# Moving the value convolution of a gated linear attention from VectorE to GpSimd

## What is computed

```python
p = h @ w_in
qkv = silu(centred_dwconv(p[..., :n_qkv], conv_w))     # 5 taps along the tokens, one weight per channel
q = l2norm(q) * DN_DK ** -0.5;  k = l2norm(k);  v = v
...
a_low = where(strict, (k * beta) @ k.T * gamma, 0)      # per chunk of 64 tokens
uw = triangular_solve(eye + a_low, [v * beta, k * beta * exp(G)])
...
for each chunk, in both directions:
    v_new = u_n - w_n @ s
    o_n = q_dec @ s + (q @ k.T * gamma) @ v_new
    s = s * exp(g_last) + k_dec.T @ v_new
```

## Time and profile before

| | us |
|---|---|
| median of 3 runs (3764.49 to 3772.21) | 3769.91 |
| the profiled execution, its own time | 3767.85 |
| its span, first to last instruction | 3766.2 |
| TensorE busy in the span | 3461.8 |
| VectorE busy | 915.3 |
| ScalarE busy | 488.1 |
| GpSimd busy | 108.7 |

### The profile page before, as it was taken

One profiled execution on the slowest core, in us unless ns is written; L12 is line 12 of the kernel. 1 busy time (PEld: TensorE's weight loads), 2 busy tenths in 40 slices (PEclk: granted clock), 3 DMA queues, 4 the chain that ended last, 5 costly groups with the idle time before them and its releaser, 6 DMA issues.

```text
span 3766.2 us, 45281 instructions
## 1 busy us (share of the span) xinstructions
PE 3461.8 (92%) x18441; PEld 2572.2 (68%) x18467; DVE 915.3 (24%) x1917; ACT 488.1 (13%) x1138; POOL 108.7 (3%) x118
## 2 busy tenths in 40 slices
PE   7999987899897997996889987789999999999998
PEld 4555665577575775775756766568888888888886
DVE  1677775300101332004740002210100000000001
ACT  1322321100001221002121011110000000000000
POOL 0111120000000000000000000000000000000000
PEclk8999999999999998998989998889999999999999
DMA  6444312253444223532013432258888888888885
GB/s 207 146 169 173 135 47 79 99 161 107 156 146 160 68 68 101 167 104 96 34 45 123 150 126 76 61 167 302 269 283 286 271 298 272 285 285 273 297 273 199
DMA packets 475303, 636.71 MB, mean 169 GB/s; under 512 B 11182, under 2 KB 419357, under 8 KB 467877
## 3 DMA queue, kind: packets, MB, share of 16 engines
q1 hardware_dynamic: 469645, 612.49, 49.0%
q0 software_dynamic: 5536, 22.51, 1.8%
HBM read 633.75 MB, written 1.20 MB: 169 GB/s over the span
## 4 chain that ended last, share of the span: by engine, by line
PE 83%; DVE 7%; DVEq 2%; issue 2%; ACT 2%; DMA 2%; PEld 1%; PEldq 1%; ACTq 0%; SPq 0%; POOL 0%
PE PS L652 37%; PE PS L660 18%; PE PS L985 4%; PE PS L2917 2%; PE PS L506 2%; PE PS L1532 2%; PE PS L1528 1%; PE PS L1868 1%; DMA WO<-in_ada_w 1%; PE PS L1114 1%; PE PS L277 1%; ACT XT L481 1%; PE PS L3156 1%; DVE scratch L1384 1%; PE PS L1525 1%
## 5 line engine op out<-in xcount | busy, mean ns | idle before, releaser
L679 DVE TENSOR_TENSOR scratch<-scratch,PS 128x128 f32<-128x128 f32 (+1 forms) x312 | 101.6, 326 | 1994.2 <-ACT scratch L669 1994.2
L652 PEld LDWEIGHTS PS<-scratch,WO 128*128 128x128 f32 x3584 | 417.8, 192 | 53.6 <-issue 53.6
L652 PEld LDWEIGHTS PS<-scratch,WF 128*128 128x128 f32 x3584 | 409.0, 192 | 24.1 <-issue 22.9
L652 PE MATMUL PS<-scratch,WO 128*128 128x128 f32 x3584 | 418.2, 275 | 0.0
L652 PE MATMUL PS<-scratch,WF 128*128 128x128 f32 x3584 | 409.2, 275 | 0.0
L660 PE MATMUL PS<-WF,scratch 128*128 128x512 f32 x832 | 382.7, 592 | 0.0
L669 ACT ACTIVATE scratch<-PS 128x128 f32<-128x128 f32 (+1 forms) x312 | 96.0, 308 | 2001.3 <-PE PS L652 2001.3
L660 PE MATMUL PS<-WO,scratch 128*128 128x512 f32 x768 | 342.1, 592 | 0.0
L652 PE MATMUL PS<-XT,WF 128*128 128x256 f32 x1536 | 338.4, 381 | 0.0
L652 PEld LDWEIGHTS PS<-XT,WF 128*128 128x128 f32 x1536 | 294.2, 192 | 49.9 <-issue 10.1
L652 PE MATMUL PS<-XT,WO 128*128 128x256 f32 x1280 | 282.8, 379 | 0.0
(11 more groups left out here) (530 smaller groups left out, 3114.0 us busy)
## 6 DMA issues: line engine op xcount, KB each, us to landing
WF<-in_moe_wg SPq DMA_DIRECT2D x56, 1024.0 KB, 5.1
WF<-in_moe_wu SPq DMA_DIRECT2D x56, 1024.0 KB, 7.6
WF<-in_moe_wd SPq DMA_DIRECT2D x56, 1024.0 KB, 4.9
WO<-in_moe_wg SPq DMA_DIRECT2D x56, 1024.0 KB, 5.1
WO<-in_moe_wu SPq DMA_DIRECT2D x56, 1024.0 KB, 7.7
WO<-in_moe_wd SPq DMA_DIRECT2D x56, 1024.0 KB, 7.3
WO<-in_ada_w SPq DMA_DIRECT2D x48, 1024.0 KB, 6.6
WF<-in_ffn_w_gate SPq DMA_DIRECT2D x18, 1024.0 KB, 5.5
```

The lines of the kernel that those rows point to most:

```text
L652: mm = nc.tensor.matmul(k.PS[:, 4 + f, w * n:(w + 1) * n], slot.gu[:, w, kb, f * P:(f + 1) * P], rhs(kb), start=kb == 0, stop=kb == KB - 1)
L679: k.nc.vector.tensor_tensor(hid[:, f, :], sg[:, f, :], k.PS[:, 4 + f, n:2 * n], ALU.mult).then_inc(*slots[s].dve.done(f"h{f}"))
```

## The change

VectorE's five instructions per head for v go away (first tap L1279, then L1281 four times). GpSimd makes the convolution in a new function, directly after `bsel`: the first tap as a product into the destination `k.cv[:, 2]`, each further tap as a product into `k.vtap` (row 6 of the output tile OT, which is free until late) and an addition. That is 9 instructions with 512 columns per head, and a drain behind each. Who waited for VectorE's `convv` (ScalarE's SiLU of v, and its copy of pv into the same raw buffer two heads later) now waits for GpSimd's. Before its first instruction GpSimd waits for the copy of pv and, for f > 0, for the transpose of the previous v; for f = 0, for the constants and for `convqk`.

```diff
--- before.py
+++ after.py
@@ -864,8 +864,8 @@
     k.gdp_act = Steps(k, "gdp_act", "pq pk pv pz")
     k.gdf_pe = Steps(k, "gdf_pe", "ssq kk qk tk tv")
     k.gdf_act = Steps(k, "gdf_act", "silu z gam eg norm v ktok vb")
-    k.gdf_dve = Steps(k, "gdf_dve", "convqk gam sq convv unit gb at qg")
-    k.gdf_pool = Steps(k, "gdf_pool", "rows bsel qt")
+    k.gdf_dve = Steps(k, "gdf_dve", "convqk gam sq unit gb at qg")
+    k.gdf_pool = Steps(k, "gdf_pool", "rows bsel convv qt")
     k.gdi_pe = Steps(k, "gdi_pe", f"g00 g01 {products} {scan_pe}")
     k.gdi_dve = Steps(k, "gdi_dve", f"pt {levels} f0 f1 {scan_dve}")
     k.gdo_pe = Steps(k, "gdo_pe", "oss")
@@ -892,6 +892,7 @@
     k.st = wf.take(2, P)
     k.rr, k.vn = s.take(2, P), s.take(2, P)
     k.os, k.osq = s.take(512), s.take(512)
+    k.vtap = k.OT[:, HEADS - 2, :]
     k.gs = [k.stage[:, 0:512].rearrange("p (n c) -> p n c", n=4), k.OT[:, HEADS - 1, :].rearrange("p (n c) -> p n c", n=4)]
     k.tmp = k.sq[:, 0, :].rearrange("p (n c) -> p n c", n=4)
     k.gdn_w = [k.WH[:, n, :].rearrange("p (kb c) -> p kb c", kb=KB) for n in range(4)]
@@ -938,6 +939,27 @@
                 elif h + 1 < ADA_HEADS:
                     ada_unit_sync(k, sp, h + 2, 0)
             gdn_weights(k, sp, h + 3, n)
+
+
+def gdn_value_gpsimd(k, pool, f):
+
+    nc = k.nc
+    cv = k.cv[:, 2, :].rearrange("p (s c) -> p s c", s=2)
+    part = k.vtap.rearrange("p (s c) -> p s c", s=2)
+    pool.wait_ge(*k.gdp_act.at("pv", f))
+    if f:
+        pool.wait_ge(*k.gdf_pe.at("tv", f - 1))
+    else:
+        pool.wait_ge(*k.pre_act.at("vecs"))
+        pool.wait_ge(*k.gdf_dve.at("convqk", f))
+    for a in range(5):
+        raw = k.raw[f % 2][:, 2, :, a:a + L]
+        i = nc.gpsimd.tensor_scalar(part if a else cv, raw, conv_col(k, a, 2, f), None, ALU.mult)
+        pool.drain()
+        if a:
+            i = nc.gpsimd.tensor_tensor(cv, cv, part, ALU.add)
+            pool.drain()
+    pool.drain().then_inc(*k.gdf_pool.done("convv"))
 
 
 def gdn_gpsimd(k, pool):
@@ -959,6 +981,7 @@
         nc.gpsimd.tensor_tensor(k.gb.rearrange("p n c -> p (n c)"), k.rows[:, 2, :], k.rows[:, 3, :], ALU.add
                                 ).then_inc(*k.gdf_pool.done("bsel"))
         pool.drain()
+        gdn_value_gpsimd(k, pool, f)
         pool.wait_ge(*k.gdf_dve.at("qg", f))
         if f >= 2:
             pool.wait_ge(*k.gdi_pe.at("os31", f - 2))
@@ -999,7 +1022,7 @@
         a = act.activation(k.zs[:, h % 3, :], bank, ACT.Copy)
     else:
         if h >= 2:
-            act.wait_ge(*k.gdf_dve.at("convv" if name == "pv" else "convqk", h - 2))
+            act.wait_ge(*(k.gdf_pool.at("convv", h - 2) if name == "pv" else k.gdf_dve.at("convqk", h - 2)))
         a = act.activation(k.raw[h % 2][:, n, :, 2:258], bank.rearrange("p (s c) -> p s c", s=2), ACT.Copy)
     a.then_inc(*k.gdp_act.done(name))
 
@@ -1231,7 +1254,7 @@
         act.wait_ge(*T.at("ssq", f))
         rsqrt(k, act, k.sq, ps[:, 6:8, :], 1.0, k.eps[:, E_RMS:E_RMS + 1]).then_inc(*S.done("norm"))
         silu_table(act)
-        act.wait_ge(*V.at("convv", f))
+        act.wait_ge(*k.gdf_pool.at("convv", f))
         act.activation(k.cv[:, v, :], k.cv[:, v, :], ACT.Silu).then_inc(*S.done("v"))
         roots_table(act)
         raw("pv")
@@ -1351,7 +1374,6 @@
         gdn_taps(k, dve, f, (0, 1), range(5), "convqk")
         gdn_decay_vector(k, dve, f)
         gdn_squares_vector(k, dve, f)
-        gdn_taps(k, dve, f, (2,), range(5), "convv")
         gdn_unit_vector(k, dve, f)
         for name in ("at", "qg"):
             gdn_grams_vector(k, dve, f, name)
@@ -1401,12 +1423,8 @@
                 gdn_decay_vector(k, dve, f)
             if h:
                 gdn_out_vector(k, dve, h - 1, "out")
-        if l == 4:
-            if front:
-                gdn_squares_vector(k, dve, f)
-                gdn_taps(k, dve, f, (2,), (0, 1))
-        if l == 5 and front:
-            gdn_taps(k, dve, f, (2,), (2, 3, 4), "convv")
+        if l == 4 and front:
+            gdn_squares_vector(k, dve, f)
         if l == 6 and front:
             gdn_unit_vector(k, dve, f)
     for half in range(2):
```

## The result

| us | before | after |
|---|---|---|
| median of 4 runs on the same chip | 3767.49 (3764.49 to 3772.21) | 3792.61 (3790.59 to 3793.32) |
| profiled execution, its own time | 3767.85 | 3793.32 |
| its span | 3766.2 | 3791.5 |

After takes 1.0065 times as long as before, with a 95% interval of 1.0047 to 1.0082: 25 us more. The forecast was 31.5 more, so the sign and the range held and the sum was some 6 us too high.

The account below looks back on a forecast made before the run. The prediction took TensorE to bound the linear attention, with VectorE late at levels 1 to 3. Its terms, 16.5 + 5.3 + 5.3 + 7 - 2.6 = 31.5 us on 3767.85, gave 3800 us, range 3772 to 3834.

Parts of the forecast that it names:

- Length and price of a product: GpSimd's 512-column product with a per-channel weight: 0.95 us long, costing VectorE 0.6 us where it meets a victim.
- its own duration less 0.35: What a GpSimd instruction costs a VectorE instruction with two SBUF inputs that it meets; 0.95 us for one of 1.3.
- rival of long products: Products of 2.08 us also fill the second stream and level 3's masks: 60 us and more, 3828 to 3850; chance 0.12.
- Price of an addition: Each GpSimd addition of 1.3 us that meets a victim costs VectorE 0.95 us.
- heads 1 to 5: Levels 1 to 3 of these heads' preparation: VectorE's held taps and masks make TensorE wait, 3.3 us each, 16.5 in all.
- first stream: First four q and k taps of a head: they meet an addition, a product and an addition, losing 2.5 us.
- second stream: Second four q and k taps: one addition left, 0.95 us, of which VectorE's idle time takes 0.7; loss 0.3.
- Solves of heads 5 and 6: Preparing heads 6 and 7: all nine cost 6.8 us, less 1.5, so 5.3 each; relief gives back 2.6 together.
- Clock: TensorE's new waits bring it to half speed: 1.2 us for each of six heads, 7 us, bounds 0 and 15.
- No transfer hangs on either: SiLU of v and `qt` start late enough and no transfer depends on them, so no term for waiting on GpSimd.
- rival in which GpSimd stays out of the way: GpSimd falls on PSUM readers and waits or is covered; loss about 2.6, gain 2.6: 3768, up to 3775; chance 0.12.
- the faster one: VectorE's relief decides under heads 5 and 6, both giving back 3.63 us, plus 1.5 of clock: 3759; chance 0.04.

Follow-up runs that it names:

- e2: The kernel before plus GpSimd's nine instructions per head, written to a spare row, VectorE's taps of v kept: 3792.12 us, 1.0063 of before.
- e4: The kernel before plus 27 drained GpSimd memsets of the spare row per head in place of the nine instructions: 3771.13 us, 1.0002 of before.
- e3: The changed kernel with only the first tap's product per head on GpSimd, the other four taps left out: 3767.75 us, 0.9993 of before.
- e11: The changed kernel with no v convolution from head 1 on, head 0 keeping one product: 3767.82 us, 0.9992 of before.
- e7: The changed kernel with GpSimd's five products per head but without its four additions: 3773.91 us, 1.0015 of before.
- e8: The changed kernel with one product per head, then four additions of the row to itself: 3791.38 us, 1.0065 of before.
- e9: The changed kernel with each product made as a two-input instruction, the weight broadcast along the columns: 3805.02 us, 1.0097 of before.
- e1: The changed kernel with GpSimd's v convolution started only behind VectorE's q and k taps in each head: 3790.40 us, 1.0054 of before.

## Why the prediction was right, and where it was off

- **Mechanism: right.** TensorE is the bound of the linear attention, levels 1 to 3 are its tight stretch, and GpSimd's reads hold VectorE's two-input instructions there. Shown: the loss is whole in e2 (no other part of the change), gone in e4 (no reads), gone in e3 (few reads). The account was not complete: VectorE's one-input instructions are held as well (1.89 us for two instead of 0.88 in e11, 1.31 for four instead of 0.86 in e4). The trace of before had it already, with 1.94 us for the same two products at 196.65, beside L954, and I did not use that row.
- **Length and price of a product: both wrong.** Taken as 0.95 us long and 0.6 dear; it is 1.57 undisturbed and 1.81 in the median, and costs 0.12 (e7; 0.25 by the whole runs). The step that failed is "its own duration less 0.35", a rule that I took from additions and masks and applied to an instruction with one tensor input. The Trainium skill (GPSIMD Engine Reference, Engine selection) says roughly line rate for one input, 0.43 us by my estimate; the trace has 1.57, longer than the two-input addition's 1.27. The 1.43 us that I called the slowest undisturbed addition was not undisturbed: VectorE's mask at 200.67 ran beside it and took 1.27 us. By the page's sentence the sum would have been 8 us lower, about 23.5, which is nearer to the result, for a reason that does not hold. My rival of long products had the length nearly right and its price wrong, so it got nothing of its time.
- **Price of an addition: right as a hold.** 0.95 said, 1.02 for the tap at 209.72. What it costs the kernel is 0.75 (after against e7) to 0.9 us (e8 against e3), and that contains the clock, which the sum had as a term of its own; the agreement of 0.9 with 0.95 is in part luck.
- **Solves of heads 0 to 4 ("heads 1 to 5"), 3.3 each, 16.5 in all: measured 2.2 each, 11.1** (idle before L1137), with 0.3 to 0.4 of busy time for groups that are broken in two. The first stream was said to lose 2.5, of which 0.6 for a product, and lost 1.45 (4.34 - 2.89): it met one addition (1.02) and one product (0.44), not two additions. The masks lost 0.5 as said. The second stream met an addition and a product and lost 1.29, less the 0.7 of idle time that I had counted: 0.6, said 0.3.
- **Solves of heads 5 and 6 ("head 6", "head 7"), 5.3 each less 2.6: measured 2.0 and 2.5 of waiting**, 4.5 for 8.0. The step is again the product: with five at 0.12 and four additions at 0.95, less my 1.5 for readers of PSUM, each comes to 2.9, and with the relief as e11 measured it (1.5 for both, said 2.6) the two come to 4.3.
- **Clock: 7 said, about 5 measured.** TensorE's busy time grew by 2.9, 1.8 and 1.6 us in the solves of heads 3, 4 and 5, 0.3 to 0.4 of each for broken groups. I had charged all six heads alike; it fell in three. The granted clock (0.95, 0.98, 0.97) shows it; in the other solves, that of head 6 apart, it is 1.00, as in before's:

```profile
331.00:404.00 73.00, 69.58 (x371) 42.09 (x371) 52.41 (x97) 19.46 (x34) 24.20 (x17) 0.95 0.44 159
404.00:477.00 73.00, 68.70 (x372) 41.66 (x372) 53.76 (x98) 19.84 (x36) 23.91 (x17) 0.98 0.37 130
477.00:544.00 67.00, 61.72 (x310) 41.63 (x310) 49.64 (x93) 20.17 (x37) 24.62 (x17) 0.97 0.15 56
```

- **"No transfer hangs on either": wrong by 1.8 us.** TensorE's waits for `in_ada_w` took up part of the delay. That makes 11.1 + 4.5 + 5.3 + 1.7 (broken groups) - 1.8 = 20.8.
- **Signs to look for.** L960 at 1.3 to 1.7: yes. L957 at 0.8 to 1.1: no. Four taps at 5 us or more: no, 4.34 (5.08 only in e8, 5.53 in e9). TensorE's wait before the second L1137 of level 2 at 3 to 4: no, it is split, 1.08 before the first and 1.15 before the second. Levels 4 to 6 no shorter, SiLU of v released by TensorE's sums: yes.

The rival in which GpSimd stays out of the way failed on the taps, the faster one on e11: even free of charge the relief is worth 1.5 us. The total came nearer to the forecast than its terms did, and that is luck: the linear attention lost 21.5 us where the sum has 31.5, and 3.8 us that no run here explains lie outside it. Open stay what in a product's 1.6 us leaves VectorE its inputs, what decides whether the clock falls, and the 3.8 us outside the linear attention.

## What to carry to other kernels

Before moving work to GpSimd, list which VectorE instructions with two SBUF inputs will run beside it and whether the bounding engine waits for them: each addition on GpSimd costs such a victim up to 1.0 us of the addition's 1.3 to 1.5, a product with a per-channel weight 0.44 at most in the rows shown, a memset nothing. Put VectorE's one-input products on the list too; here they were held even by memsets. Relief of an engine that isn't the bound is worth little (here 1.5 us of 25 taken off), and moving the collisions only helps as far as VectorE has idle time at the new place (a loss of 25 us became one of 12 to 15, never 0).

## What the runs showed of the hardware

- GpSimd's `tensor_scalar` with a weight per partition on 128x512 takes 1.57 us undisturbed, its two-input addition 1.27, and the same product with a broadcast second input 1.04 to 1.31 (e9).
- A product held the tap at 207.80 for 0.44 us and let it end first; an addition, or a product with a broadcast input, holds a tap until 0.55 us after its own end (209.72 in after, 213.27 in e9).
- VectorE's `tensor_scalar` (one input tensor) is held as well: four of 128x128 took 1.31 us beside memsets (e4) and 1.88 in e1 against 0.86, two of 128x512 1.89 beside a GpSimd mask against 0.88 (e11).
- Being held is mutual: additions take up to 2.13 us against 1.27 alone.
- The same waits, 1.82 + 0.66 and 1.81 + 0.66 us, left TensorE at 2.4 GHz in the solve of head 2 and were followed by half speed in that of head 3; nothing in the rows shown tells the two apart. At such waits the clock is a matter of chance for a prediction, and a bound rather than a term.
